# Spreading gates and roots over the partitions: transposes of a repeated column in place of products of diagonal tiles with ones

## The chip, the cores and the metric

The kernel runs on one core of a Trainium2 chip. TensorE multiplies matrices from SBUF into PSUM; VectorE, ScalarE and GpSimd (POOL in the profile) do elementwise work; SyncE issues most DMA transfers. The engines run their own instruction streams and wait for one another by semaphores. The metric is the time of one execution on the device in microseconds (us). Before the change the median of three runs is 1413.25 us (1412.88 to 1413.94).

## The reference, cut to what matters

Two layers over 512 tokens of width 1024. Layer 0 has a gated DeltaNet mixer, layer 1 a sparse attention over latents; each mixer is followed by a SwiGLU feed-forward part (FFN). Around every one of the four sub-layers stands

```python
h = rms_norm(x, norm_g[layer, 0]) * (1.0 + sc_m) + sh_m
y = mixer(h)                                             # gdn_mixer or dsa_mixer
x = x + (1.0 + ga_m) * rms_norm(y, norm_g[layer, 1])     # ga_m: a gate for each of the 1024 columns
h = rms_norm(x, norm_g[layer, 2]) * (1.0 + sc_f) + sh_f
y = swiglu(h, ffn_w_in[layer], ffn_w_out[layer])
x = x + (1.0 + ga_f) * rms_norm(y, norm_g[layer, 3])
```

and in the sparse attention the two latents (256 wide, for the queries and for the keys) are normed:

```python
c_q = rms_norm(c_q, q_norm_g)
c_kv = rms_norm(c_kv, kv_norm_g)      # rsqrt(mean of squares) for each token
```

## The kernel before, in words

Activations that feed a product with weights stand with the model's columns on the partitions (tiles h_hi, h_lo: 128 partitions, 8 chunks, 512 tokens). Every large product is done three times in the fp32r format, high x high, high x low and low x high, where ScalarE rounds the weights to the high part (w_hi, line 379), VectorE subtracts to get the low part (w_lo, line 385). Weights come in quads of four tiles, two transfers of 1 MB each, into two buffers `raw`.

The sub-layers' outputs stand the other way round, tokens on the partitions, 1024 columns along the free axis. The gate (1 + ga) * norm_g of a sub-layer is worked out as `coef`, with the columns on the partitions: 8 values on each of 128 partitions. To multiply it to an output it is needed as a row of 1024 values, the same on every partition. That tile is `CB[m]`, for sub-layer m = 0 (DeltaNet), 1 (its FFN), 2 (attention), 3 (its FFN). It is made in three steps: `dve_cdiag` builds eight 128x128 diagonal tiles on VectorE (identity times coef), `pe_cb` multiplies them with a matrix of ones on TensorE, two fp32 products of 512 columns into two PSUM banks, and `act_cb` copies these to SBUF on ScalarE.

The same is done with the roots of the latents. `dve_var` takes the mean squares of 4 blocks of tokens (128x4), `pool_root` raises them to the power -0.5 on GpSimd, `dve_var` then builds four diagonal tiles in `diag`, and `pe_bcast` multiplies them with ones: one fp32 product of 512 columns. `latent_dve` (line 2366) multiplies the latent with the result. Here the tokens stand on the partitions at first and are needed along the free axis.

The order of all work is written out by hand, one stream for each engine. m = 0 is spread in the last steps of the DeltaNet input projection (step 30 of 32), m = 1 behind the first part of the first FFN, m = 2 and m = 3 at the end of `pe_out(1)` and `pe_out(2)`. There the last block of tokens is turned (transposes of xs, line 740), ScalarE makes the last quarter of h_hi from it (line 803, then 809), and `pe_last_tokens` (lines 434 to 446) goes on with the next weights on these tokens, waiting for `h_rounded`. The two roots are spread in `dsa_in_pe`, the first behind the small projection (lines 2129 to 2131), the second between the indexer's logits (line 2197) and its scores (line 2209).

Of the kernel before, what the change touches and what calls it, by code (L numbers as in the profile page):

```python
# [19 lines left out]
P = 128  # L20
# [58 lines left out]
def build_trunk(nc, x, c, ada_w, ada_b, norm_g, ffn_w_in, ffn_w_out,  # L79
# [31 lines left out]
    with ExitStack() as ctx:  # L111
# [15 lines left out]
        class Region:  # L127
# [3 lines left out]
            def __call__(self, name, shape, dt=F32):  # L131
                size = 4
                for n in shape[1:]:
# [33 lines left out]
        row_rinv = fixed("row_rinv", [P, 2, NB])  # L167
        row_stat = fixed("row_stat", [P, 2, NB, 2])
        ada_acc = fixed("ada_acc", [P, 512])
        h_base = place[0]  # L170
        h_hi = fixed("h_hi", [P, DC, S], F32R)
        h_lo = fixed("h_lo", [P, DC, S], F32R)
# [52 lines left out]
        y_ffn = ffn("y_ffn", [P, NB, D])  # L225
        silu_g = ffn("silu_g", [P, 2, S])
        gated = tmp[:, 0:2, :]
        cdiag_ffn = fixed("cdiag_ffn", [P, DC, P], at=ffn.at)
        late_ffn = [ffn(f"late_ffn{i}", [P, 2, 1024], F32R) for i in range(2)]


# [46 lines left out]

        CB = [cb_gdn, cb_late, cb_late, cb_late]
        LATE = [late_gdn, late_ffn, late_dsa, late_ffn]  # L280
        CDIAG = [state[:, :, :], cdiag_ffn[:, :, :], silu_g[:, :, :].rearrange("p a (b n) -> p (a b) n", n=P),
                 p_t[:, 0, :, :].rearrange("p a (b n) -> p (a b) n", n=P)]

        qi_t = fixed("qi_t", [P, 4, S], at=h_base)
        mask = fixed("mask", [P, NB, S], at=h_base + 8192)
        v_tok = fixed("v_tok", [P, NB, 1024], at=h_base + 16384)
# [32 lines left out]
        def flat(t):  # L319
            return t.rearrange("p a b -> p (a b)")  # L320
# [239 lines left out]
        def dve_var(dve, n, width=D):  # L560
            dve.wait_ge(sem("stat_made"), n + 1)
            nc.vector.tensor_scalar(var[:, 0:NB], ps[:, 4, 0:NB * P:P], 1.0 / width, EPS,
                                    ALU.mult, ALU.add).then_inc(sem("row_made"), 1)
            dve.wait_ge(sem("row_root"), 1 + 16 + n + 1)
            nc.vector.tensor_tensor(diag[:, :, :], over_heads(ident[:, :]), along(rinv[:, 0:NB]),
                                    ALU.mult).then_inc(sem("x_diag"), 1)

        def pool_root(pool, n):
            pool.wait_ge(sem("row_made"), 1 + 16 + n + 1)
            nc.gpsimd.tensor_tensor(rinv[:, 0:NB], var[:, 0:NB], half[:, 0:NB], ALU.pow)\  # L570
                .then_inc(sem("row_root"), 1)

        def pe_bcast(pe, n):
            pe.wait_ge(sem("x_diag"), diag_no(1, NB - 1) + n + 1)
            nc.tensor.matmul(ps[:, ROOT_BANK[n], :], ones[:, :], flat(diag[:, :, :]), start=True, stop=True)\
                .then_inc(sem("root_out"), 1)

        def act_first(act):

# [106 lines left out]

            act_split(act, q, s, free=(tile_done, 4 * (q - 2) + s + 1))

        def dve_cdiag(dve, m, tile, layer):
            nc.vector.tensor_tensor(tile, over_heads(ident[:, :], DC), along(coef[:, layer, 1 + 2 * (m % 2), :]),  # L690
                                    ALU.mult).then_inc(sem("x_diag"), 1)

        def pe_cb(pe, m, bank0):

            src = CDIAG[m].rearrange("p (a b) n -> p a (b n)", a=2)
            pe.wait_ge(sem("x_diag"), 2 if m == 0 else diag_no(m - 1, NB - 1) + 1 if m == 1 else diag_no(m - 1, -1))
            for j in range(2):
                last = nc.tensor.matmul(ps[:, bank0 + j, :], ones[:, :], src[:, j, :], start=True, stop=True)
            last.then_inc(sem("h_mm"), 1)

        def act_cb(act, m, bank0):
# [12 lines left out]

        def diag_no(m, b):

            return 3 + 6 * m + b + (1 if m >= 2 else 0)

        def turn_no(m, b, g):

# [774 lines left out]
        def gdn_slot_dve(dve, ch, n):  # L1495

            if n == 6:
                dve_gates_made(dve, ch)
            if n == 10:
                dve_k_sums(dve)  # L1500
            if n == 11:
                dve_factors(dve, ch)
            if n == 13:
                dve_negc(dve)
            dve_ada_slot(dve, ch, n)
            if not TO_GATES <= n < TO_QUERIES:
                dve_conv(dve, ch, n)
            if n < N_TILES - 4:
                dve_split(dve, n // 4 + 1, n % 4)
            else:  # L1510
                out_split(dve, nc.vector, 0, Q_GDN_OUT, n % 4)
            if n == 4:
                dve_gates_in(dve, ch)
            if n == 5:
                dve_gates_mid(dve, ch)
            if n == 7:
                dve_g_sums(dve, ch)
            if 13 <= n < 17:
                dve_l(dve, 2 * (n - 13))
                dve_l(dve, 2 * (n - 13) + 1)  # L1520
            if n == 16:
                dve_diagonals(dve)
            if n in ELIMINATE:
                dve_eliminate(dve, ch, ELIMINATE[n])
            if n == 23:
                dve_diagonals_out(dve)
                dve_inverses_out(dve)
            if n == 25:
                quarter_w_out(dve, dve_copy, 1)
            if n == 26:  # L1530
                quarter_z_out(dve, dve_copy, 1)
                dve_inverse_turned(dve)
            if n == 27:
                half_w_out(dve, dve_copy, 1)
                half_w_out(dve, dve_copy, 3)
            if n == 28:
                half_z_out(dve, dve_copy, 1)
                half_z_out(dve, dve_copy, 3)
            if n == 29:
                dve.wait_ge(sem("half_mm"), 2)  # L1540
                dve_cdiag(dve, 0, state[:, :, :], 0)

        def gdn_slot_pe(pe, n):

# [411 lines left out]
        def ffn_dve(dve, ch, layer):  # L1956
            m = 1 + 2 * layer
            for p in range(3):
                q, n, c0 = part_quads(layer, p)
                j0 = 10 + 6 * p  # L1960

                def epilogue(i, s, split):
                    ci = i + c0
                    if s < 2:
                        split(s)
                        return
                    dve.wait_ge(tile_done, i * 4 + 4 * q + s + 1)
                    dve.wait_ge(sem("ffn_silu"), ci * 2 + s - 1)
                    nc.vector.tensor_tensor(gated[:, s - 2, :], silu_g[:, s - 2, :], ps[:, s, :], ALU.mult)\  # L1969
                        .then_inc(sem("ffn_mul"), 1)  # L1970
                    split(s)
                    dve.wait_ge(sem("ffn_hi"), ci * 2 + s - 1)
                    one = bass.ds(i * 2 + s - 2, 1)
                    nc.vector.tensor_tensor(flat(g_lo[:, one, :]), gated[:, s - 2, :], f32(flat(g_hi[:, one, :])),
                                            ALU.subtract).then_inc(sem("ffn_lo"), 1)

                def ada(i, s):
                    if layer == 0 and not (p == 2 and i == 2):
                        dve_ada_beside(dve, ch, i + j0, s, first=j0 if p == 0 else None)

                def body(i):
                    for s in range(4):
                        ada(i, s)
                        epilogue(i, s, lambda s: dve_split(dve, i + q + 1, s))

                repeat(dve, n - 1, body, ch)
                for s in range(4):
                    ada(n - 1, s)
                    if layer == 0 and p == 0 and s == 1:
                        dve_coef(dve, ch, 0, [3])  # L1990
                        dve_cdiag(dve, 1, CDIAG[1], 0)
                    if layer == 0 and p == 2 and s == 1:
                        dve_ada_out(dve, ch, 23)
                        dve_coef(dve, ch, 1, [0, 1, 2, 3])
                    epilogue(n - 1, s, lambda s: half_split(dve, q + n, s))
                if p == 2:
                    for s in range(4):
                        out_split(dve, nc.vector, m, q + n + 1, s)
                    if layer == 0:
                        dve_cdiag(dve, 2, CDIAG[2], 1)  # L2000
                    dve.wait_ge(y_out, Y_FFN[layer] + 16)
                    break
                y0 = Y_FFN[layer] + 8 * p
                for j in range(2):
                    nxt = (lambda s: half_split(dve, q + n + 1, s)) if j == 0 else \
                        (lambda s: dve_split(dve, q + n + 2, s))
                    for b in range(4):
                        if layer == 0:
                            dve_ada_beside(dve, ch, 14 + 6 * p + j, b)
                        if b == 3:  # L2010
                            for s in range(3):
                                nxt(s)
                        dve_y(dve, layer, p, q + n + j, b, j, y0 + 4 * j + b, p > 0)
                    nxt(3)
# [696 lines left out]
        def _(dve):  # L2711
# [52 lines left out]
            dve.wait_ge(lo_done, 4 * Q_DSA_OUT + 4)  # L2764
            for s in range(4):
                out_split(dve, nc.vector, 2, Q_DSA_OUT + 1, s)
            dve_cdiag(dve, 3, CDIAG[3], 1)
            dve_out(dve, 2, lambda s: dve_split(dve, Q_FFN[1], s))
            ffn_dve(dve, ch, 1)
            dve_out(dve, 3, None)  # L2770
# [49 lines left out]
```

## Time and profile before

| | |
|---|---|
| median of three runs | 1413.25 us |
| profiled execution, its own time | 1411.94 us |
| its span, first to last instruction | 1410.3 us |
| TensorE busy | 1347.9 us, 96% |
| VectorE busy | 811.5 us, 58% |
| ScalarE busy | 570.0 us, 40% |
| GpSimd busy | 124.3 us, 9% |
| mean granted TensorE clock | 0.99 |

The span lies within the time of its execution, which has 1.64 us around it. Busy time of TensorE is that of matmuls, whose ends are modelled, and which overlap with the next ones: a record that lasts 0.40 us can stand 0.23 us behind the one before. What a group of matmuls costs is thus read from the chain of waits, where pieces stand end to end, and not from the sum of their durations.

### The profile page before, as it was taken

How to read it: one execution, taken by the hardware profiler on the slowest of the kernel's cores; microseconds unless marked ns; L12 is line 12 of the kernel's file. 1: busy time of each engine (PE TensorE's matmuls, PEld its weight loads, DVE VectorE, ACT ScalarE, POOL GpSimd, SP SyncE). 2: the span in 40 equal slices, each digit the busy share in tenths (PEclk: the TensorE clock that was granted, in tenths of full speed). 3: DMA queues.
4: the chain of work that ended last, by engine and by line, in shares of the span. 5: the costliest groups of instructions: out<-in, count | busy, mean ns of one | idle time of the engine just before them, and what ended most of it. 6: DMA issues, size and time to landing. Idle time of an engine off the chain costs nothing.

```text
span 1410.3 us, 18287 instructions
## 1 busy us (share of the span) xinstructions
PE 1347.9 (96%) x7071; PEld 1088.3 (77%) x7071; DVE 811.5 (58%) x1398; ACT 570.0 (40%) x1085; POOL 124.3 (9%) x142
## 2 busy tenths in 40 slices
PE   3899998999999999999999999999999999999998
PEld 3678887889787877887888865665888888888886
DVE  4977877457476655555556759776563323333335
ACT  3265865345443212221224654686353213222231
POOL 0002020016100000000000003030000000000000
PEclk9899999999999999999999999999999999999999
DMA  9555322111335555555532121010122223222321
GB/s 325 189 180 177 123 90 81 40 61 67 114 98 201 179 179 179 179 178 179 179 120 90 56 58 33 28 54 8 61 90 89 89 90 118 91 90 66 113 90 60
DMA packets 102855, 158.39 MB, mean 112 GB/s; under 512 B 9325, under 2 KB 74106, under 8 KB 102778
## 3 DMA queue, kind: packets, MB, share of 16 engines
q1 hardware_dynamic: 91898, 115.40, 24.9%
q0 software_dynamic: 10880, 41.95, 8.7%
q8 instruction: 50, 0.82, 0.2%
q14 instruction: 27, 0.22, 0.0%
HBM read 155.24 MB, written 2.10 MB: 112 GB/s over the span
## 4 chain that ended last, share of the span: by engine, by line
PE 83%; DVE 8%; ACT 5%; issue 2%; DMA 1%; SPq 0%; POOL 0%; DVEq 0%; POOLq 0%; ACTq 0%
PE ps L401 13%; PE ps L402 13%; PE ps L403 13%; PE ps L2070 4%; PE ps L2072 4%; PE ps L2071 4%; PE ps L761 3%; PE ps L763 3%; PE ps L762 3%; DVE ada_acc L504 1%; DVE w_lo L385 1%; PE ps L523 1%; PE ps L2442 1%; PE ps L2467 1%; PE ps L2209 1%
## 5 line engine op out<-in xcount | busy, mean ns | idle before, releaser
L401 PE MATMUL ps<-h_hi,w_hi 128*128 128x512 f32 x872 | 348.4, 400 | 0.0
L403 PE MATMUL ps<-h_hi,w_lo 128*128 128x512 f32 x872 | 344.7, 395 | 0.0
L402 PE MATMUL ps<-h_lo,w_hi 128*128 128x512 f32 x872 | 344.7, 395 | 0.0
L385 DVE TENSOR_TENSOR w_lo<-raw,w_hi 128x1024 fp32r<-128x1024 f32 x172 | 208.9, 1220 | 233.9 <-ACT w_hi L379 233.4
L379 ACT ACTIVATE w_hi<-raw 128x1024 fp32r<-128x1024 f32 x174 | 182.3, 1050 | 147.2 <-PE ps L2072 143.0
L403 PEld LDWEIGHTS ps<-h_hi,w_lo 128*128 128x128 f32 x872 | 164.5, 189 | 38.9
L402 PEld LDWEIGHTS ps<-h_lo,w_hi 128*128 128x128 f32 x872 | 164.6, 189 | 37.9 <-issue 0.5
L401 PEld LDWEIGHTS ps<-h_hi,w_hi 128*128 128x128 f32 x872 | 164.6, 189 | 37.9 <-issue 0.5
L504 DVE SCALAR_TENSOR_TENSOR ada_acc<-ada_in,c_act,ada_acc 128x512 f32<-128x512 f32 x154 | 115.5, 750 | 4.1
L1934 ACT ACTIVATE g_hi<-tmp 128x512 fp32r<-128x512 f32 x44 | 27.8, 632 | 209.1 <-DVE tmp L1969 209.1
L2070 PE MATMUL ps<-w_hi,g_hi 128*128 128x512 f32 x256 | 101.6, 397 | 2.6 <-DVE w_lo L385 2.6
L2072 PE MATMUL ps<-w_hi,g_lo 128*128 128x512 f32 x256 | 101.1, 395 | 0.0
L2071 PE MATMUL ps<-w_lo,g_hi 128*128 128x512 f32 x256 | 101.0, 395 | 0.0
L1929 ACT ACTIVATE silu_g<-ps 128x512 f32<-128x512 f32 x44 | 26.2, 596 | 147.8 <-PE ps L403 138.4
L1049 DVE SCALAR_TENSOR_TENSOR tmp<-conv_u,conv_t,tmp 128x512 f32<-128x512 f32 x72 | 54.1, 752 | 43.2 <-ACT tmp L1043 41.2
L1969 DVE TENSOR_TENSOR tmp<-silu_g,ps 128x512 f32<-128x512 f32 x44 | 30.3, 688 | 59.4 <-PE ps L403 58.9
L366 POOL DMA_DIRECT2D ada_in<-in_ada_w_dram x40 | 30.4, 759 | 385.7 <-DVE ada_acc L504 348.4
L2070 PEld LDWEIGHTS ps<-w_hi,g_hi 128*128 128x128 f32 x256 | 48.1, 188 | 14.7 <-DVE w_lo L385 3.5
L2072 PEld LDWEIGHTS ps<-w_hi,g_lo 128*128 128x128 f32 x256 | 48.1, 188 | 11.5
L2071 PEld LDWEIGHTS ps<-w_lo,g_hi 128*128 128x128 f32 x256 | 48.2, 188 | 11.1
L965 POOL TENSOR_TENSOR row_rinv<-row_var,half 128x1 f32<-128x1 f32 x16 | 8.7, 545 | 510.2 <-DVE row_var L894 510.1
L2557 DVE CUSTOM_DVE_ANT_0 s_m<-ps,mask 128x128 f32<-128x128 f32 (+3 forms) x64 | 28.9, 487 | 23.8 <-PE ps L2467 23.3
(392 smaller groups left out, 2151.3 us busy)
## 6 DMA issues: line engine op xcount, KB each, us to landing
raw<-in_ffn_w_in_dram SPq DMA_DIRECT2D x44, 1024.0 KB, 5.2
ada_in<-in_ada_w_dram POOLq DMA_DIRECT2D x40, 1024.0 KB, 5.6
raw<-in_ffn_w_out_dram SPq DMA_DIRECT2D x20, 1024.0 KB, 5.1
raw<-in_gdn_w_in_dram SPq DMA_DIRECT2D x16, 1024.0 KB, 5.8
ada_in<-in_ada_w_dram SPq DMA_DIRECT2D x4, 1024.0 KB, 9.4
x_t<-in_x_dram SPq DMA_DIRECT2D x2, 2048.0 KB, 9.8
early_slab<-in_ada_w_dram SPq DMA_DIRECT2D x4, 1024.0 KB, 14.2
raw<-in_gdn_w_out_dram SPq DMA_DIRECT2D x4, 1024.0 KB, 4.9
```

What stands on the lines that cost most here:

```text
L379: nc.scalar.activation(split_tile(w_hi, s, kc) if dst is None else dst(w_hi), raw_tile(s, kc) if src is None else src, ACT.Copy).then_inc( ...
L385: ops.tensor_tensor(lo, raw_tile(s, kc) if src is None else src, f32(hi), ALU.subtract).then_inc(lo_done, 1)
L401: nc.tensor.matmul(out_, hi[:, k, :], r_hi[:, k, :], start=k == 0, stop=False)
L402: nc.tensor.matmul(out_, hi[:, k, :], r_lo[:, k, :], start=False, stop=False)
L403: last = nc.tensor.matmul(out_, lo[:, k, :], r_hi[:, k, :], start=False, stop=k == kc - 1)
L504: ins = nc.vector.scalar_tensor_tensor(ada_sum(j)[:, :], slab_place(j)[b][:, k, :], cc, ada_sum(j)[:, :], ALU.mult, ALU.add)
L761: nc.tensor.matmul(ps[:, to, :], s_hi[:, k, toks], hi[:, cols], start=k == 0, stop=False)
L762: nc.tensor.matmul(ps[:, to, :], s_hi[:, k, toks], lo[:, cols], start=False, stop=False)
L1049: ins = nc.vector.scalar_tensor_tensor(conv_a[n % 2], conv_u[n % 2][:, j:j + S], conv_t[:, j, channel(n):channel(n) + 1], conv_a[n % 2], A ...
L2070: nc.tensor.matmul(ps[:, b, :], g_hi[:, k, toks], hi, start=k == 0, stop=False)
L2071: nc.tensor.matmul(ps[:, b, :], g_hi[:, k, toks], lo, start=False, stop=False)
L2072: last = nc.tensor.matmul(ps[:, b, :], g_lo[:, k, toks], hi, start=False, stop=k == PARTS[p] - 1)
```

## The change

The eight values of a gate are copied to a small tile `gates` (`dve_gate`, 128x8), and `pe_cb` transposes, eight times, one column of it repeated 128 times (a read with step 0): the result has that column as each of its rows. For a root, `pe_bcast` does the same with the four columns of `rinv`, as GpSimd leaves them; the two latents have their own columns of it now, and TensorE waits for GpSimd. The diagonal tiles, and the VectorE instructions that build them, are gone. The counts of the semaphore `x_diag` (`diag_no`) follow from that. The new tile of 128 bytes on each partition stands before h_hi, so later tiles move by as much.

```diff
+        gates = fixed("gates", [P, 4, DC])
...
-        CDIAG = [state[:, :, :], cdiag_ffn[:, :, :], silu_g[:, :, :].rearrange("p a (b n) -> p (a b) n", n=P),
-                 p_t[:, 0, :, :].rearrange("p a (b n) -> p (a b) n", n=P)]
...
         def dve_var(dve, n, width=D):
...
-            dve.wait_ge(sem("row_root"), 1 + 16 + n + 1)
-            nc.vector.tensor_tensor(diag[:, :, :], over_heads(ident[:, :]), along(rinv[:, 0:NB]),
-                                    ALU.mult).then_inc(sem("x_diag"), 1)
 
         def pool_root(pool, n):
             pool.wait_ge(sem("row_made"), 1 + 16 + n + 1)
-            nc.gpsimd.tensor_tensor(rinv[:, 0:NB], var[:, 0:NB], half[:, 0:NB], ALU.pow)\
+            nc.gpsimd.tensor_tensor(rinv[:, NB * n:NB * n + NB], var[:, 0:NB], half[:, 0:NB], ALU.pow)\
                 .then_inc(sem("row_root"), 1)
 
         def pe_bcast(pe, n):
-            pe.wait_ge(sem("x_diag"), diag_no(1, NB - 1) + n + 1)
-            nc.tensor.matmul(ps[:, ROOT_BANK[n], :], ones[:, :], flat(diag[:, :, :]), start=True, stop=True)\
-                .then_inc(sem("root_out"), 1)
+            pe.wait_ge(sem("row_root"), 1 + 16 + n + 1)
+            for b in range(NB):
+                last = nc.tensor.transpose(ps[:, ROOT_BANK[n], b * P:(b + 1) * P],
+                                           rinv[:, NB * n + b:NB * n + b + 1].to_broadcast([P, P]), ident[:, :])
+            last.then_inc(sem("root_out"), 1)
...
-        def dve_cdiag(dve, m, tile, layer):
-            nc.vector.tensor_tensor(tile, over_heads(ident[:, :], DC), along(coef[:, layer, 1 + 2 * (m % 2), :]),
-                                    ALU.mult).then_inc(sem("x_diag"), 1)
+        def dve_gate(dve, m):
+            nc.vector.tensor_copy(gates[:, m, :], coef[:, m // 2, 1 + 2 * (m % 2), :]).then_inc(sem("x_diag"), 1)
 
         def pe_cb(pe, m, bank0):
 
-            src = CDIAG[m].rearrange("p (a b) n -> p a (b n)", a=2)
             pe.wait_ge(sem("x_diag"), 2 if m == 0 else diag_no(m - 1, NB - 1) + 1 if m == 1 else diag_no(m - 1, -1))
-            for j in range(2):
-                last = nc.tensor.matmul(ps[:, bank0 + j, :], ones[:, :], src[:, j, :], start=True, stop=True)
+            for d in range(DC):
+                last = nc.tensor.transpose(ps[:, bank0 + d // 4, d % 4 * P:(d % 4 + 1) * P],
+                                           gates[:, m, d:d + 1].to_broadcast([P, P]), ident[:, :])
             last.then_inc(sem("h_mm"), 1)
...
-            return 3 + 6 * m + b + (1 if m >= 2 else 0)
+            return 3 + 6 * m + b - (1 if m >= 2 else 0)
```

The four calls of `dve_cdiag(dve, m, ...)` become `dve_gate(dve, m)` at the same places.

How TensorE's stream stands at the gate m = 0, before. An `x2` behind a row counts instructions of one kind in a row; the moving operand is named first, then the stationary one.

```order
L403 MATMUL ps<-h_hi,w_lo 128x512
L1077 MATMUL ps<-ones,diag 128x1 x4
L698 MATMUL ps<-state,ones 128x512 x2
L401 MATMUL ps<-h_hi,w_hi 128x512
L402 MATMUL ps<-h_lo,w_hi 128x512
```

And after; the lines of the changed kernel are lower by a few.

```order
L400 MATMUL ps<-h_hi,w_lo 128x512
L1072 MATMUL ps<-ones,diag 128x1 x4
L692 MATMUL ps<-ident,gates 128x128 x8
L398 MATMUL ps<-h_hi,w_hi 128x512
L399 MATMUL ps<-h_lo,w_hi 128x512
```

The two products are replaced in place, and nothing around them moves. The second root on TensorE, before, with the logits ahead of it and the scores behind:

```order
L2177 MATMUL ps<-ident,kn 128x128 x4
L550 MATMUL ps<-ones,sq_lat 128x128 x8
L2197 MATMUL ps<-kn_t,qi_t 128x256 x8
L575 MATMUL ps<-diag,ones 128x512
L2209 MATMUL ps<-relu,w_diag_158 128x256 x8
```

And after:

```order
L2172 MATMUL ps<-ident,kn 128x128 x4
L547 MATMUL ps<-ones,sq_lat 128x128 x8
L2192 MATMUL ps<-kn_t,qi_t 128x256 x8
L570 MATMUL ps<-ident,rinv 128x128 x4
L2204 MATMUL ps<-relu,w_diag_158 128x256 x8
```

One product becomes four transposes, at the same place. VectorE at the first root, before:

```order
L385 TENSOR_TENSOR w_lo<-raw_62,w_hi 128x1024
L562 TENSOR_SCALAR var<-ps 128x4
L565 TENSOR_TENSOR diag<-ident,rinv 128x512
L385 TENSOR_TENSOR w_lo<-raw_62,w_hi 128x1024
L2366 SCALAR_TENSOR_TENSOR tmp<-ps,vec_t,latent 128x512 x2
```

And after:

```order
L382 TENSOR_TENSOR w_lo<-raw_61,w_hi 128x1024
L382 TENSOR_TENSOR w_lo<-raw_62,w_hi 128x1024
L559 TENSOR_SCALAR var<-ps 128x4
L382 TENSOR_TENSOR w_lo<-raw_62,w_hi 128x1024
L2361 SCALAR_TENSOR_TENSOR tmp<-ps,vec_t,latent 128x512 x2
```

The build of the diagonal tiles is gone from between the mean squares and the next split.

## Rows read from the trace of the kernel before

**Rows 1.** The page: busy time of the engines, and the chain that ended last.
```profile
PE 1347.9 (96%) x7071; PEld 1088.3 (77%) x7071; DVE 811.5 (58%) x1398; ACT 570.0 (40%) x1085; POOL 124.3 (9%) x142
...
PE 83%; DVE 8%; ACT 5%; issue 2%; DMA 1%; SPq 0%; POOL 0%; DVEq 0%; POOLq 0%; ACTq 0%
```
**Rows 2.** The chain of waits at m = 0 and 1: start us, us on the chain, what.
```profile
284.90 1.82 PE ps L698 x4
...
539.00 1.72 PE ps L698 x4
```
**Rows 3.** The chain of waits at 1006 us, transposes among full matmuls.
```profile
1006.55 0.87 PE ps L740 x8
```
**Rows 4.** Single lines: engine, operation, count: duration ns min/median/max, first and last start us.
```profile
L698 PE MATMUL ps<-state,ones x4: 592/592/676, 284.8 to 286.1; 128*128 128x512 f32 x4
...
L740 PE MATMUL ps<-ident,xs x96: 270/272/301, 372.0 to 1037.7; 128*128 128x128 f32 x96
...
L1164 PE MATMUL ps<-upto,gate x64: 273/275/356, 115.3 to 140.9; 128*128 128x128 f32 x64
...
L690 DVE TENSOR_TENSOR state<-ident,coef x1: 1219/1219/1219, 282.3 to 282.3; 128x1024 f32<-128x1024 f32 x1
```
**Rows 5.** Timeline, TensorE at 115 us: start us, length us, engine, line, what.
```profile
115.31 2.03 PE L1164 MATMUL ps<-upto,gate 128*128 128x128 f32 x16
```
**Rows 6.** Timeline behind m = 0; in brackets: idle time before, what ended it.
```profile
293.55 2.33 DVE L1049 SCALAR_TENSOR_TENSOR tmp<-conv_u,conv_t,tmp 128x512 f32<-128x512 f32 x3 [4.72 <-ACT tmp L1043]
```
**Rows 7.** TensorE's waits from 540 to 760 us: total us, times, longest.
```profile
PE ps L2070 <- DVE w_lo L385: 1.3, 1, 1.3
```
**Rows 8.** Timeline at m = 2 and 3, and one later start on an empty array.
```profile
795.53 1.50 ACT L803 ACTIVATE h_hi<-ps,mod,coef 128x128 fp32r<-128x128 f32 x4 [0.81 <-PE ps L740]
...
797.18 0.59 PE L434 MATMUL ps<-h_hi,w_hi 128*128 128x256 f32 x1
...
810.45 0.37 PE L434 MATMUL ps<-h_hi,w_hi 128*128 128x256 f32 x1
...
1037.53 1.50 ACT L803 ACTIVATE h_hi<-ps,mod,coef 128x128 fp32r<-128x128 f32 x4 [0.58 <-PE ps L740]
...
1039.18 0.59 PE L434 MATMUL ps<-h_hi,w_hi 128*128 128x256 f32 x1
```
**Rows 9.** The chain of waits at the two roots.
```profile
819.98 0.87 PE ps L575 x2
820.88 0.76 DVE tmp L2366
...
835.33 1.05 PE ps L575 x2
```
**Rows 10.** Timeline around the two roots.
```profile
813.43 0.69 DVE L565 TENSOR_TENSOR diag<-ident,rinv 128x512 f32<-128x512 f32 x1 [1.12 <-POOL rinv L570]
...
829.65 0.66 PE L2177 MATMUL ps<-ident,kn 128*128 128x128 f32 x4
...
833.41 0.69 DVE L565 TENSOR_TENSOR diag<-ident,rinv 128x512 f32<-128x512 f32 x1 [1.12 <-POOL rinv L570]
...
836.43 1.41 DVE L2366 SCALAR_TENSOR_TENSOR tmp<-ps,vec_t,latent 128x512 f32<-128x512 f32 x2 [2.32 <-PE ps L575]
```
**Rows 11.** Timeline behind VectorE's builds for m = 1 and m = 2.
```profile
477.67 0.17 DVE L538 SCALAR_TENSOR_TENSOR coef<-mod,vec_t 128x8 f32<-128x8 f32 x1
...
481.49 1.22 DVE L385 TENSOR_TENSOR w_lo<-raw,w_hi 128x1024 fp32r<-128x1024 f32 x1 [2.40 <-ACT w_hi L379]
...
758.78 1.46 DVE L878 TENSOR_TENSOR y_ffn<-y_ffn,ps 128x512 f32<-128x512 f32 x2
...
767.69 1.03 PE L740 MATMUL ps<-ident,xs 128*128 128x128 f32 x8
```
**Rows 12.** Stretches: from:to, length, busy us (x records) by engine, granted clock, DMA share, GB/s.
```profile
300.00:305.00 5.00, 4.83 (x30) 4.54 (x29) 1.45 (x3) 1.63 (x5) 0.00 (x0) 0.66 0.28 116
...
767.00:769.00 2.00, 2.00 (x14) 1.77 (x13) 1.32 (x3) 1.11 (x3) 0.00 (x0) 1.00 0.00 0
```

More of the change, by code:

```diff
@@ L227, in build_trunk @@
         gated = tmp[:, 0:2, :]
-        cdiag_ffn = fixed("cdiag_ffn", [P, DC, P], at=ffn.at)
         late_ffn = [ffn(f"late_ffn{i}", [P, 2, 1024], F32R) for i in range(2)]
@@ L1540, in gdn_slot_dve @@
                 dve.wait_ge(sem("half_mm"), 2)
-                dve_cdiag(dve, 0, state[:, :, :], 0)
+                dve_gate(dve, 0)
         def gdn_slot_pe(pe, n):
@@ L1990, in ffn_dve @@
                         dve_coef(dve, ch, 0, [3])
-                        dve_cdiag(dve, 1, CDIAG[1], 0)
+                        dve_gate(dve, 1)
                     if layer == 0 and p == 2 and s == 1:
@@ L1999, in ffn_dve @@
                     if layer == 0:
-                        dve_cdiag(dve, 2, CDIAG[2], 1)
+                        dve_gate(dve, 2)
                     dve.wait_ge(y_out, Y_FFN[layer] + 16)
@@ L2766, in _ @@
                 out_split(dve, nc.vector, 2, Q_DSA_OUT + 1, s)
-            dve_cdiag(dve, 3, CDIAG[3], 1)
+            dve_gate(dve, 3)
             dve_out(dve, 2, lambda s: dve_split(dve, Q_FFN[1], s))
```

## The prediction, made before the result was known

> **What bounds the kernel now.** I read the page first. TensorE is busy 96% of the span and carries 83% of the chain that ended last; VectorE carries 8% [rows 1]. So an edit on TensorE counts almost wherever it lies in a full stretch, and one on VectorE only where VectorE is the last to arrive. The change touches six places: four where a gate is spread (m = 0 near 285 us, m = 1 near 539, m = 2 near 796, m = 3 near 1038) and two where a root is spread (near 820 and 835). Next I read the chain of waits there. It holds the four records of the two ones-products as pieces of TensorE's own work, with TensorE's work right before and behind: 1.82 us for m = 0, 1.72 for m = 1 [rows 2]. Then I read eight fp32 transposes of 128x128 that stand among full matmuls: 0.87 us for the eight [rows 3]. Last I read the timeline at each place for what else must be there before TensorE can go on.
>
> **What replaces what on TensorE.** An fp32 product of 512 columns leaves two records of 592 ns each; an fp32 transpose of 128x128 leaves one record of 272 ns, and these overlap, since eight of them take 0.87 us on the chain, 0.109 each [rows 3, 4]. A gate had two products and gets eight transposes; a root had one product and gets four transposes. What no row shows is a transpose whose stationary operand is one column read 128 times. The nearest are plain fp32 products with such an operand (gate, line 1164): 275 ns a record [rows 4], and sixteen of them take 2.03 us together [rows 5], (2.03 - 0.27) / 15 = 0.117 from start to start, against the transposes' 0.109. I therefore take 0.109 each.
>
> **Place m = 0.** 1.82 - 0.87 = 0.95 us. Does it reach the end? Behind it comes the last projection tile, TensorE without a gap. Then ScalarE evicts it, and VectorE's convolution begins after 4.72 us of waiting for that [rows 6]. Both would start as much earlier as TensorE ends. From there a chain through all engines begins that hangs on this tile. So 0.95 counts; the low end is 1.82 - 1.03 = 0.79, if the eight cost their whole length from first start to last end (1.03, the transposes at 767.69 [rows 11]).
>
> **Place m = 1.** 1.72 - 0.87 = 0.85 us, again between full tiles. Behind it there is one wait of 1.3 us for VectorE's split in the next 220 us [rows 7]. The split that ends it stands behind VectorE's work on the gated products, which TensorE's last tiles release, so I take the wait to move along with TensorE. Low end 0.69.
>
> **Places m = 2 and m = 3.** Here the saving is mostly hidden. The next matmul (line 434) reads the last quarter of the tokens in h_hi, whose first four chunks ScalarE makes in four activations: 795.53 + 1.50 = 797.03, and 1037.53 + 1.50 = 1039.03. TensorE's first matmul behind the product starts at 797.18 and 1039.18 [rows 8], 0.15 us after ScalarE. It is the activations that release it, now and afterwards. The product only keeps the array filled a little longer: the matmul ends at 797.77, where one that starts on an empty array needs 0.37 us (the row at 810.45 [rows 8]) and would end at 797.55. I count 0.2 us each, from 0 to 0.85 each. What is late next is ScalarE, and it gains nothing by the change.
>
> **The roots.** At the first, TensorE is full until 819.98 and the product takes 0.87; VectorE takes up the result 0.03 us later and the latents' chain hangs on that [rows 9]. Four transposes take half of 0.87, so 0.43 is saved; if they cost what four others took from start to end, 0.66 (829.65 [rows 10]), 0.21. At the second the product takes 1.05 [rows 9], and VectorE has waited 2.32 us for it [rows 10]: I take 0.50, between 0.39 (against 0.66) and 0.61 (against 0.44). The scores right behind it (line 2209) read relu tiles that ScalarE has made by then but for the last, which is needed at their end, so TensorE can use the time.
>
> **VectorE.** Gone are four diagonal builds of 1.22 us and two of 0.69; added are four copies of 128x8, for which the nearest row is an operation on 128x8 at 0.17 us [rows 4, 10, 11]. That is 6.3 - 0.7 = 5.6 us less, and I cost it at nothing. Behind the build at 477.87 VectorE waits 2.40 us for a rounded weight [rows 11], so the time is only added to that wait; the builds for m = 0 and m = 3 stand before similar waits. The build for m = 2 is followed at once by the sum at 758.78, which could now start earlier, but the product of this ends in the transposes at 767.69, and TensorE comes to them without a wait [rows 11]. The second root's build runs from 833.41 to 834.10 [rows 10]; TensorE arrives at 835.33 [rows 9], 1.2 us later. The first root's starts at 813.43 [rows 10], over 6 us before its product. TensorE now waits for the power of GpSimd instead, which ends before the build began. No wait is added, and no queue is passed.
>
> **The sum.** 0.95 + 0.85 + 0.20 + 0.20 + 0.43 + 0.50 = 3.13 us. The low ends give 0.79 + 0.69 + 0 + 0 + 0.21 + 0.39 = 2.1, the high ones 0.95 + 0.85 + 0.85 + 0.85 + 0.43 + 0.61 = 4.5. The profiled execution took 1411.94 us (span 1410.3), so it would take 1408.8. It lies 1.3 us under the median of the three runs, and I put the change on the median: 1413.25 - 3.1 = 1410.1 us, 0.22% less. What a measurement of this kernel can tell from no change is about 0.2%, that is 2.8 us: the forecast sits almost on that edge, at 1410.4.
>
> The Trainium skill (TensorE: Matmul & The Clock Gate, Terms) calls the transpose mode "4× faster for FP32". This case's rows give 1.72 against 0.87 us for the same 1024 columns, a factor of 2. By the page's factor the eight would take 0.43 us and the sum would be 4.4 us instead of 3.1; by the rows they do not.
>
> **Rivals.**
> First, the saving does not pass on from m = 0 or m = 1. For it: both lie in stretches where transfers of 1 MB are under way and VectorE's splits set the pace for short times. Against it: TensorE has one wait in the 220 us behind m = 1 [rows 7]. If both are lost, the rest is 1.3 us: 1411.9.
> Second, the forecast is too careful: ScalarE is not what releases line 434, and places m = 2 and 3 give their full 0.85. That adds 1.3 us: 1408.8. Against it, the two starts lie 0.15 us behind ScalarE's end in both places.
> Third, slower: transposes of a repeated column do not overlap, each costing its own length of 0.272 us [rows 4]. There are 40 of them, and the products they replace take 1.82 + 3 x 1.72 + 0.87 + 1.05 = 8.9 us. 40 x 0.272 - 8.9 = 2.0 us more: 1415.2. It decides from 8.9 / 40 = 0.22 us each, and it leaves the 0.2% band from 0.29. Against it: the transposes of xs do overlap, and so do the records with a repeated column [rows 5].
> The Trainium skill (TensorE: Matmul & The Clock Gate, Part 4: PE-mode transpose) speaks for this rival: it gives about 275 ns for a transpose within a kernel, most of it access latency. The trace agrees on the length of one (272) and not on what eight in a row cost.
> Fourth, the clock: in the stretch from 300 to 305 us, behind a pause of TensorE, the granted clock is 0.66 [rows 12], which is some 3.4 us at 1.2 instead of 2.4 GHz, a loss of 1.7 us of work. Were that to follow the new transposes once or twice, 1411.8 to 1413.5. Against it: with eight transposes in the stretch at 767 the clock stays at 1.00 [rows 12], and at every place dense matmuls stand on both sides.
> The same section says that the clock gate does not count transposes as work; with one microsecond of them in a row no row here shows an effect.
>
> **How the numbers follow.** Forecast 0.64; first rival (one or both) 0.18; second 0.07; third 0.04; clock 0.04; something unseen, such as the 128 bytes by which every later tile moves, 0.03. Within the forecast I give 0.62 to a time below 1410.4, since its terms are from rows and half of the spread lies on either side. So faster by over 0.2%: 0.64 x 0.62 + 0.07 = 0.47. Slower by over 0.2%: part of the third and of the unseen, 0.04. The rest, 0.49, is within 0.2%. The range: from 1408.4 (nearly the sum's high end, 4.5, and 0.3 for the runs' own spread) to 1412.8 (the first rival with both places lost, and 0.9 for the clock or the spread).
>
> **What the new profile would show.** Eight records behind one another in about 1.0 us at the four gates, four in some 0.6 at the roots, 40 in all, one record each and not two. Line 434's successor still starts 0.15 us behind ScalarE's four activations, after a short pause of TensorE that is not there now. VectorE's waits are longer by what was taken from it. The convolution of the last projection tile starts 0.95 us earlier, and the first attention top-k about 3 us earlier. I am wrong if the transposes lie more than 0.2 us apart, if each leaves two records, or if TensorE's waits grow between 293 and 540 us by about what m = 0 saved.

## The result, and the profile after

The changed kernel takes 1395.37 us (median of three executions, 1392.86 to 1397.77) against 1413.25 before, a ratio of 0.9873 with a 95% interval of 0.986 to 0.9886: 17.9 us less, where 3.1 were forecast and the range ended at 1408.4. A second session with other executions gave 1398.36, ratio 0.9901 (0.9886 to 0.9915).

The places of the change do what was forecast. This is the chain of waits after, at the gates m = 0 and m = 1 and at the two roots (start us, us on the chain, what); it answers to [rows 2, 3, 9].

```profile
286.48 0.93 PE ps L692 x8
...
538.14 0.87 PE ps L692 x8
...
814.06 0.45 PE ps L570 x4
...
830.22 0.58 PE ps L570 x4
```

1.82 became 0.93, 1.72 became 0.87, 0.87 became 0.45 and 1.05 became 0.58: 2.63 us together, where the sum had 2.73. At m = 2 and m = 3 TensorE now waits for ScalarE's four activations, as the timeline at m = 2 shows (answering to [rows 8]; at m = 3 the wait is 0.38 us too):

```profile
789.57 1.50 ACT L798 ACTIVATE h_hi<-ps,mod,coef 128x128 fp32r<-128x128 f32 x4 [0.82 <-PE ps L735]
...
791.22 0.35 PE L431 MATMUL ps<-h_hi,w_hi 128*128 128x256 f32 x1 [0.38 <-ACT h_hi L798]
```

789.57 + 1.50 = 791.07, and the matmul starts 0.15 us later and takes 0.35. So the six places give their 3 us of TensorE's work, and 15 us come from elsewhere. The page of after shows from where:

```profile
PE 1330.0 (95%) x7091; PEld 1094.0 (78%) x7091; DVE 807.1 (58%) x1396; ACT 570.1 (41%) x1085; POOL 124.3 (9%) x142
...
L398 PE MATMUL ps<-h_hi,w_hi 128*128 128x512 f32 x872 | 343.6, 394 | 0.4 <-ACT tmp L1038 0.4
...
L400 PE MATMUL ps<-h_hi,w_lo 128*128 128x512 f32 x872 | 340.2, 390 | 0.0
```

And the same lines of the page before (busy us, mean ns of one behind the first bar):

```profile
L401 PE MATMUL ps<-h_hi,w_hi 128*128 128x512 f32 x872 | 348.4, 400 | 0.0
L403 PE MATMUL ps<-h_hi,w_lo 128*128 128x512 f32 x872 | 344.7, 395 | 0.0
```

These matmuls were not touched, and each is 5 to 6 ns shorter. Summed over the 3384 matmuls of lines 401 to 403 and 2070 to 2072 that is 18 us of busy time. TensorE's whole busy time fell by 17.9 us [rows 1]. A stretch of the second FFN, where TensorE is full, shows it as a rate: in 100 us it does 431 matmuls before and 443 after (the columns are those of [rows 12]).

```profile
1150.00:1250.00 100.00, 100.00 (x431) 80.42 (x430) 32.38 (x34) 26.11 (x32) 0.00 (x0) 1.00 0.29 95
```
```profile
1150.00:1250.00 100.00, 100.00 (x443) 82.81 (x442) 34.57 (x38) 29.27 (x36) 0.00 (x0) 1.00 0.29 95
```

The clock is 1.00 in both. From the start of one 512-column matmul to the start of the next, at full clock, the traces have 232.3 ns before and 227.2 after, on average over 4200 pairs. The difference is there before 285 us already (232.5 against 227.8), ahead of any instruction that the change touches.

Part of this is given back. The mean granted clock of the profiled execution is 0.985, against 0.990:

```profile
core 0: 1396.1 us, clock 0.985
```

(1 - 0.985) x 1396 - (1 - 0.990) x 1410 = 6.8 us of clock lost. With 18.0 won at those untouched matmuls and 3.1 at the six places, 14.3 should be left, and the span fell from 1410.3 to 1396.1, by 14.2. That it fits to 0.1 us is luck: some 600 more untouched matmuls gained as well, and not every microsecond of lost clock costs time, as the runs with other pads show below.

**Where to look for the reason.** The new tile moves h_hi and all behind it by 128 bytes, and leaves x_t, w_hi, w_lo and the rest ahead of it in place. By the sizes in the code, the start of h_hi lies 59776 bytes behind that of w_hi in a partition, 233 x 256 + 128. After, they are 59904 apart, 234 x 256. The trace of before has both kinds of distance in it. In the output product of the attention (lines 761 to 763) the weights are the moving operand. The first of them come from w_hi and w_lo, ahead of the place of the new tile, and the others from late_dsa, behind it like the stationary tile o_t_hi. The view of line 761 in that stretch (duration ns min/median/max):

```profile
L761 PE MATMUL ps<-late_dsa,o_t_hi x16: 389/389/393, 1012.8 to 1029.5; 128*128 128x512 f32 x16
L761 PE MATMUL ps<-w_hi,o_t_hi x14: 390/393/482, 1008.7 to 1024.1; 128*128 128x512 f32 x14
```

One line of code, one shape, 389 or 393 ns, by where the moving tile lies. Start to start it is 227.0 against 232.3 ns. Taken over the whole trace of before, some 4000 pairs of matmuls that read w_hi or w_lo together with a tile behind the place have 232.6 ns, and the 321 pairs whose two tiles both lie behind it have 228.2. After, both forms of the line are at 389:

```profile
L756 PE MATMUL ps<-late_dsa,o_t_hi x15: 389/389/389, 1008.7 to 1024.5; 128*128 128x512 f32 x15
L756 PE MATMUL ps<-w_hi,o_t_hi x8: 389/389/476, 1014.2 to 1019.1; 128*128 128x512 f32 x8
```

### The profile page after: what moved, and what is told of

Its sections match the earlier page's. It is cut to its first block, busy times and chain, and to the rows that moved or that the text cites. A ratio compares the mean times of both kernels' runs of the same rounds, so it can differ in the third digit from the quotient of the medians.

```text
span 1396.1 us, 18325 instructions
## 1 busy us (share of the span) xinstructions
PE 1330.0 (95%) x7091; PEld 1094.0 (78%) x7091; DVE 807.1 (58%) x1396; ACT 570.1 (41%) x1085; POOL 124.3 (9%) x142
## 4 chain that ended last, share of the span: by engine, by line
PE 81%; DVE 9%; ACT 5%; issue 2%; DMA 1%; SPq 0%; POOL 0%; DVEq 0%; POOLq 0%; ACTq 0%
PE ps L398 13%; PE ps L400 13%; PE ps L399 13%; PE ps L2065 4%; PE ps L2067 4%; PE ps L2066 4%; PE ps L756 3%; PE ps L758 3%; PE ps L757 3%; DVE w_lo L382 2%; DVE ada_acc L501 1%; PE ps L520 1%; PE ps L2437 1%; ACT w_hi L376 1%; PE ps L2124 1%
## 5 line engine op out<-in xcount | busy, mean ns | idle before, releaser
L398 PE MATMUL ps<-h_hi,w_hi 128*128 128x512 f32 x872 | 343.6, 394 | 0.4 <-ACT tmp L1038 0.4
L400 PE MATMUL ps<-h_hi,w_lo 128*128 128x512 f32 x872 | 340.2, 390 | 0.0
L399 PE MATMUL ps<-h_lo,w_hi 128*128 128x512 f32 x872 | 339.9, 390 | 0.0
```

What stands on the lines that cost most here:

```text
L398: nc.tensor.matmul(out_, hi[:, k, :], r_hi[:, k, :], start=k == 0, stop=False)
L399: nc.tensor.matmul(out_, hi[:, k, :], r_lo[:, k, :], start=False, stop=False)
L400: last = nc.tensor.matmul(out_, lo[:, k, :], r_hi[:, k, :], start=False, stop=k == kc - 1)
```

## The experiments

Two theories are set against each other. Theory A: the time of a matmul depends on the distance between the addresses of its stationary and its moving tile. Theory B: the transposes, or the VectorE work that is gone, let TensorE run faster elsewhere.

**1. The pad alone.** The kernel before with unused bytes where the change has its gates.

```diff
         ada_acc = fixed("ada_acc", [P, 512])
+        pad = fixed("pad", [P, 32])
```

> The kernel before with an unused tile of 128 bytes ahead of h_hi, where the change puts its gates; no instruction differs. Theory A (distance of addresses): a matmul whose stationary and moving tile lie on either side of that place has its two addresses apart by 128 modulo 256 bytes in the kernel before and by 0 after, and stands 232.5 ns behind the one before instead of 227. The 3500 such matmuls then cost about 17 us less: 1398 us, or 1395 to 1400, and the start-to-start of lines 401 to 403 is 227 ns. Theory B (the transposes did it, by what they leave behind on TensorE): 1413 us, 232.5 ns.

Measured: 1396.98 us (1395.58 to 1397.42) against 1412.84, ratio 0.9891 (0.9876 to 0.9905), and 227.3 ns from start to start. No instruction differs from the kernel before, so theory B falls as the cause of the large part, and 128 unused bytes give 15.9 us. For some 4000 matmuls 5.1 ns each would be 20 us (an estimate from the traces' averages). Part of it goes to a clock of 0.987 against 0.989 or 0.990.

**2. The change without the move.**

```diff
-        gates = fixed("gates", [P, 4, DC])
+        gates = half[:, 32:64].rearrange("p (a b) -> p a b", a=4)
```

> The changed kernel with its gates in the unused half of the tile of constants, so that no tile moves. Theory A: only what the transposes save themselves, 3.1 us by the forecast's sum: 1410 us, start-to-start 232.5 ns. Theory B: 1395 us, 227 ns, and more stretches of lower clock than in the kernel before.

Measured: 1412.98 us (1408.59 to 1417.37, 12 executions), ratio 1.0003 (0.9989 to 1.0018); 232.4 ns. The twelve fall into two groups: six from 1408.59 to 1411.03 with a mean granted clock of 0.990 or 0.991, six from 1414.93 to 1417.37 with 0.983 to 0.987. The first group's median, 1409.1, is 3.7 us below the kernel before, whose clock is 0.989 or 0.990 in nearly all executions. The second lies 7 us higher, which is about what 0.005 less clock over 1412 us comes to. The groups were formed after the times were known, by time and clock together. The profiled execution is of the first group, and its chain of waits has the forecast's pieces:

```profile
285.52 0.93 PE ps L692 x8
...
536.71 0.87 PE ps L692 x8
...
816.93 0.45 PE ps L570 x4
...
832.93 0.58 PE ps L570 x4
```

So the transposes save some 3 us of work and, over all executions, no time that these runs can tell from none.

**3. A pad ahead of the weights.** w_hi, w_lo and all behind them move together.

```diff
+        pad = fixed("pad", [P, 32])
         raw = [fixed(f"raw{i}", [P, 8, 256]) for i in range(2)]
```

> The kernel before with the unused 128 bytes ahead of the raw and rounded weights, so that w_hi and w_lo move together with all tiles behind them. Theory A in its form with a distance between the two operands: the distance is as before, 1413 us and 232.5 ns. Theory A in the other form, that h_hi itself has a better address: 1398 us, 227 ns. Theory B: 1413 us.

Measured: 1413.08 us, ratio 1.0002 (0.9993 to 1.0011), 232.3 ns. h_hi lies as in the fast kernels and gains nothing by it: with both tiles moved by 128 bytes all stays as it was, so it is the distance between them and not the place of h_hi.

**4. The change again**, on the chip and in the session of the first three.

> The changed kernel once more, for a second trace on the same chip as the others. Both theories: 1395 us. If the stretches of lower clock near 818 us and 978 us come from the transposes at the roots and gates, they are here and in the kernel with the gates in the tile of constants, and not in the padded kernel before; if they come from the faster pace, they are here and in the padded one.

Measured: 1398.36 us (1395.96 to 1398.89). With the transposes the time is 1.4 us above that of the pad alone, and not 3 below; the ranges of the four executions each overlap. Both have stretches of lower clock. The view of stretches, first the changed kernel, then the padded one:

```profile
976.40:979.80 3.40, 3.40 (x8) 2.75 (x9) 2.61 (x4) 0.63 (x1) 0.00 (x0) 0.50 0.02 5
815.90:819.30 3.40, 3.40 (x10) 2.62 (x9) 2.19 (x8) 1.11 (x3) 1.01 (x1) 0.51 0.04 8
297.10:303.90 6.80, 5.76 (x26) 5.50 (x27) 2.04 (x3) 2.51 (x9) 0.00 (x0) 0.50 0.34 139
```
```profile
976.60:980.00 3.40, 3.40 (x10) 2.62 (x9) 2.70 (x4) 0.63 (x1) 0.00 (x0) 0.51 0.02 5
816.20:819.60 3.40, 3.40 (x9) 2.67 (x9) 2.19 (x8) 1.85 (x5) 1.01 (x1) 0.50 0.02 5
297.10:303.90 6.80, 4.59 (x40) 4.34 (x40) 2.43 (x5) 3.45 (x11) 0.00 (x0) 1.00 0.44 154
```

The two late ones, at 1.2 GHz, do not need the transposes. Of these two executions only the changed kernel's has the one at 297 us, but that one does not need the transposes either. Experiment 3, where no instruction differs from the kernel before, has such a stretch:

```profile
303.10:309.90 6.80, 6.15 (x30) 5.85 (x29) 2.50 (x4) 2.21 (x8) 0.00 (x0) 0.50 0.07 28
```

The kernel before has 3.4 us of it at 300.4 us.

**5 to 8. How the distance counts.** Other sizes of the pad of experiment 1.

```diff
-        pad = fixed("pad", [P, 32])
+        pad = fixed("pad", [P, 96])    # 64, 16 and 8 in the others
```

> The kernel before with 384 unused bytes ahead of h_hi: stationary and moving tile are then apart by 256 modulo 512 and by 0 modulo 256. If the distance counts modulo 256: 227 ns from start to start and 1397 us. If modulo 512 or more: 232.5 ns and 1413 us.

> 256 unused bytes: apart by 128 modulo 512, and by 128 modulo 256 as in the kernel before. Modulo 256: 232.5 ns, 1413 us, no change. If any pad near 128 bytes or above helps (a theory of room, not of distance): 1397 us.

> 64 unused bytes: apart by 192 modulo 256. If only a distance of 0 modulo 256 is fast: 232 ns, 1413 us. If the cost grows with the distance from a multiple of 256: about 229 to 230 ns, 1405 us.

> 32 unused bytes: apart by 160 modulo 256. If only a distance of 0 modulo 256 is fast: 232 ns, 1413 us. If the cost grows with the distance: about 231 ns, 1409 us.

| pad ahead of h_hi, bytes | w_hi to h_hi, modulo 256 | start to start, ns | time, us | ratio (interval) |
|---|---|---|---|---|
| 0 (before) | 128 | 232.3 | 1412.8 to 1414.0 | 1 |
| 32 | 160 | 233.6 | 1420.55 | 1.0045 (1.0021 to 1.0068) |
| 64 | 192 | 231.8 | 1414.16 | 1.0003 (0.9992 to 1.0015) |
| 128 | 0 | 227.3 | 1396.98 | 0.9891 (0.9876 to 0.9905) |
| 256 | 128 | 232.3 | 1413.64 | 1.0 (0.9988 to 1.0011) |
| 384 | 0 | 227.2 | 1395.91 | 0.988 (0.984 to 0.992) |
| 128, ahead of w_hi too | 128 | 232.3 | 1413.08 | 1.0002 (0.9993 to 1.0011) |

Of the distances that were tried, those that are equal modulo 256 bytes give the same time: 0 and 256 bytes of pad, and 128 and 384. Of the four values modulo 256 only 0 is fast. The version in which the cost grows with the distance is refuted: 64 bytes from a multiple (the pad of 64) costs 4.6 ns a matmul, and 128 cost 5.1. The pad of 32 did worse than either theory expected of it; 1.3 ns more for each of some 4000 matmuls are 5 us of the 6.6 that it is slower than the kernel before in its session. Its clock of 0.986 against 0.990 would by itself come to 5.6 us more, so both together overshoot, and clock lost on TensorE reaches the time only in part.

**9. The roots alone, nothing moved.** The diff of `dve_var`, `pool_root`, `pe_bcast` and `diag_no`, without that of the gates.

> The kernel before with transposes at the two roots alone, no tile moved. By the forecast's terms 0.4 + 0.5 = 0.9 us less: 1412.1 us, if no other stretch of TensorE is granted the lower clock. If the shift of what follows brings such stretches (1.7 us of work lost in each of 3.4 us at half), the runs spread from 1412 to 1416.

Measured: 1416.16 us (1412.92 to 1418.11), ratio 1.0019 (1.0008 to 1.003): slower than before, although it only takes work away. Even the two executions with a clock of 0.989 or 0.990 took 1412.92 and 1413.51, about as the kernel before (1413.04). The profiled execution (1415.36 us) has a stretch behind the first root, 6.8 us long, that the kernel before does not have:

```profile
822.90:829.70 6.80, 6.10 (x14) 4.79 (x15) 5.14 (x14) 1.75 (x5) 1.01 (x1) 0.50 0.17 29
```

It does not need the transposes: experiment 7, which has none, shows 6.8 us at 1.2 GHz from 823.2 us. That the earlier end of the root brought it here is thus not shown.

**10. The gates alone, nothing moved.** `dve_gate` and `pe_cb` as in the change, the roots as before.

> The kernel before with transposes at the four gates alone, no tile moved. By the forecast's terms 0.95 + 0.85 + 0.2 + 0.2 = 2.2 us less: 1410.7 us in executions whose clock is as in the kernel before (0.990), and up to 7 us more in those with 0.984. If the whole spread of the version with both comes from the roots, there is none here.

Measured: 1412.74 us (1408.45 to 1414.94, 12 executions), ratio 0.9992 (0.9982 to 1.0001). The spread is here too, so it does not come from the roots alone: the four executions under 1410.5 have a clock of 0.990 or 0.993, the one at 1414.94 has 0.985.

**11. Work in the pause.** If TensorE's pause of 2.2 us behind the first root brings the lower clock, work whose result nobody reads should prevent it. Two fp32 products into a PSUM bank that is free there:

```diff
             last.then_inc(sem("small_turned"), 1)
+            for _ in range(2):
+                nc.tensor.matmul(ps[:, 4, :], ones[:, :], x_t[:, 0, 0:S], start=True, stop=True)
```

> The changed kernel with two fp32 products of ones and x into a free PSUM bank, in TensorE's pause of 2.2 us behind the first root; their result is read by nobody. If the pause is what brings the stretch of lower clock at 818 us, it is gone, TensorE's first product behind the pause starts at the same time, and 0 to 1.7 us are saved: 1396.5 us. If the clock falls there for another reason, it stays and the time is 1398 us or a little more.

Measured: 1394.95 us (1393.46 to 1397.03), ratio 0.9872 (0.9858 to 0.9886). The pause of the changed kernel and the stretch behind it:

```profile
814.90:817.70 2.80, 0.62 (x5) 0.47 (x5) 2.73 (x5) 1.26 (x2) 0.00 (x0) 1.00 1.21 199
817.70:821.10 3.40, 3.40 (x9) 2.65 (x8) 2.24 (x8) 0.97 (x3) 0.96 (x1) 0.50 0.02 5
```

and with the filling work:

```profile
816.00:820.00 4.00, 3.97 (x17) 3.27 (x18) 2.74 (x9) 1.77 (x5) 1.01 (x1) 1.00 0.12 20
```

In the one execution that was traced there is no stretch of lower clock, as expected. That the filling work did it is not shown. Experiment 5 has the same pause unfilled, 2.60 us long, and no such stretch behind it either. This is its view, the pause first:

```profile
813.80:816.40 2.60, 0.04 (x1) 0.00 (x0) 2.54 (x4) 1.26 (x2) 0.00 (x0) 1.00 1.20 196
816.40:819.80 3.40, 3.36 (x15) 2.81 (x16) 2.57 (x8) 1.17 (x3) 0.61 (x1) 1.00 0.02 5
```

Of the twelve traces in which the pause behind the first root is not filled (it lasts 2.2 or 2.6 us in all of them), eight have a stretch of 3.4 or 6.8 us at 1.2 GHz that begins within 1.5 us of the pause's end, and four have none: the kernel before and experiments 3, 5 and 6. The two traces with the filling work have none. With a share of four in twelve, two such traces in a row come about by chance one time in nine. The median is 3.4 us below that of experiment 4, but the two were run on different chips, their ranges overlap, and three of the four executions have the clock of 0.985 that experiment 4 has. So no gain in time is shown either.

**12. The pad and the filling work, without the change.** Experiments 1 and 11 together.

> The kernel before with the 128 unused bytes and the same two products behind the first root, whose diagonal tiles are kept. As above: no lower clock near 816 us, 1395.5 us against 1397.0 of the padded one. Between this and the version above stands what the transposes give once tiles lie well: by the forecast's sum 3 us for the transposes, by the runs so far nothing.

Measured: 1393.97 us (1393.01 to 1397.69), ratio 0.9873 (0.9858 to 0.9887), clock 0.991 in the profiled execution, and 1.00 at the place. That execution has no lower clock at 297, 355 or 976 us either, where nothing was filled, so its absence at 816 us says little on the filling:

```profile
816.00:820.00 4.00, 4.00 (x19) 3.31 (x18) 2.71 (x10) 2.68 (x7) 1.01 (x1) 1.00 0.02 4
```

Beside experiment 11, in the same session, the transposes again show no gain: 1394.95 with, 1393.97 without, four executions each. This version has none of the change's instructions, beats the kernel before by 1.3%, and stands level with the changed one.

## Why the prediction was wrong, by its own steps

**The step that failed** is the one that was given 0.03: "something unseen, such as the 128 bytes by which every later tile moves". It named the right thing, but as one guess among the unseen, without a price in the sum or the range. The sum treated all matmuls outside the six places as fixed. What the runs showed in its place: the 128 bytes alone, without any change of an instruction, take 5.1 ns from the start-to-start time of some 4000 matmuls, and 15.9 us from the kernel (experiment 1). The evidence lay in the trace of before, in durations of one line with moving tiles on either side of the place (393 against 389 ns); I read that line only for where it stands, not for its two forms.

**Replacement on TensorE: right.** A transpose of a repeated column takes 272 ns as a record and 0.11 us in a row, one record each, and not two. The third rival (no overlap) is refuted. The Trainium skill (TensorE: Matmul & The Clock Gate, Part 4: PE-mode transpose) gives about 275 ns for a transpose. The length of a record here agrees (272 ns), but eight in a row take 0.87 to 0.93 us, and not the 2.2 us that an estimate of eight times that figure gives. The Trainium skill (TensorE: Matmul & The Clock Gate, Terms) also calls the transpose mode "4× faster for FP32", without saying than what; against the products with ones it is a factor of 2 here, 1.72 to 0.87 us.

**m = 0 and m = 1: right in size** (0.89 and 0.85 where 0.95 and 0.85 were forecast). Whether it all reaches the end is open. The prediction's own sign of being wrong is there: between 293 and 540 us TensorE's waits come to 7.8 us before and to 8.8 in experiment 2, a growth of about what m = 0 saved. But with the pad alone, where m = 0 saves nothing, they come to 9.2, so this sign does not tell the one from the other.

**m = 2 and m = 3: right.** ScalarE releases the next matmul, 0.15 us behind its last activation, and TensorE waits 0.38 us for it. The matmul ends 0.50 us behind the activations, where it was 0.74 before: 0.24 us saved, where 0.2 were forecast. The second rival is refuted.

**The roots: right in size** (0.42 and 0.47 where 0.43 and 0.50 were forecast).

**VectorE: right as far as the runs tell.** The six builds are gone (6.3 us), the four copies take 0.16 to 0.17 us each, and TensorE's time shows no gain by it.

**The sum of 3.13: right as work, wrong as time.** With tiles unmoved the six executions at the old clock are 3.7 us faster and the other six 3.5 us slower. The fourth rival, the clock, was priced too low and bound to the wrong thing. It asked whether transposes would lower the clock where they stand. What happens is that stretches at 1.2 GHz near 297, 355, 820 and 978 us are there in some executions and kernels and not in others, with and without the transposes, and that they can outweigh 3 us of work. Experiment 9 has 0.9 us less work and 3 us more time. The stretches near 300, 355 and 820 us stand close to a pause of TensorE (1.4, 2.0 and 2.2 to 2.6 us long). That a pause is their cause, or that a small shift of the work ahead of them turns them on or off, would fit and is not shown: the same pause of 2.6 us is followed by full clock in four traces. What decides it for a given execution is open.

**What stays open** is also why the distance counts. A conjecture that fits is that the weights of the next matmul are read while the moving tile of this one streams, and that the two reads meet. No experiment took the reads apart.

## What to carry to other kernels

Before a small allocation is judged by what it holds, work out what it moves: here 128 bytes ahead of a tile are worth five times what the change they came with was forecast to give. In a profile, compare the forms of one matmul line (same shape, other tiles); if their durations differ by a few ns, try the tiles' distance, and test any change of layout with a version that has the pad alone and one that has the edit alone. A saving of a few us in a kernel full of TensorE work can be less than what one or two more stretches of lower clock cost (1.7 us of work for each 3.4 us at half clock), so a verdict on it needs the clock of each execution beside its time.

## What the runs showed of the hardware that was not expected

- In this kernel, an fp32r matmul of 128x128 by 512 columns in a full stream starts 227.2 ns behind the one before when the addresses of w_hi and h_hi, its stationary and its moving tile, differ by a multiple of 256 bytes (experiments 1 and 5). It is 231.8, 232.3 or 233.6 ns when they differ by 192, 128 or 160 modulo 256 (experiments 7, 6 and 8). Moving both tiles by 128 bytes changes nothing (experiment 3).
- At 128 modulo 256 the times from start to start follow a pattern that comes again in almost the same form every seven matmuls (240, 233, 231, 231, 229, 230, 232, then 241, 233, 230, 232, 228, 230, 233 ns, in the trace of before behind 1100 us), where at 0 they are 226 or 227.
- The clock granted to TensorE fell to 1.2 GHz for 3.4 or 6.8 us near the end of a pause of 2.2 or 2.6 us in eight of twelve traces, with dense work ahead of the pause, and stayed full in the other four. In the two traces in which 1.9 us of unused products filled the pause it stayed full too (experiments 11 and 12), which is too few to say that the filling did it.
- A kernel with 0.9 us less work for TensorE was 0.2% slower (experiment 9, 1.0008 to 1.003); the cause is open.
